# Order of VectorE, of the weight splits and of the last output projection in a two-block transformer kernel

## The reference, cut to what matters

```python
# first block: an even layer (Fourier mix and differential attention), an odd layer (short conv)
x = x + gate0 * (concat(fourier, attention) * silu(g)) @ even_w_out
h = rms_norm(x) ...; bg, cg, xt, g = split(h @ odd_w_in)
x = x + gate1 * (bg * conv3(cg * xt) * silu(g)) @ odd_w_out
# second block: an RG-LRU branch y_a and an HGRN2 branch y_b over one input projection
h = rms_norm(x); xa, ga, q, f, v, g, m_a, m_b = split(h @ w_in)
y = sigmoid(m_a) * y_a + sigmoid(m_b) * rms_norm(hgrn2(silu(q), f, v)) * silu(g)
x = x + y @ w_out
x = x + square(relu(rms_norm(x) @ w_up)) @ w_down
return rms_norm(x)
```

## Time and profile before

| | |
|---|---|
| median of 3 runs | 3000.41 us (2998.44 to 3001.2) |
| the profiled execution's own time | 3001.18 us |
| its span, first to last instruction | 2999.1 us |
| TensorE matmuls busy in the span | 2866.4 us (96%) |
| VectorE, ScalarE, GpSimd busy | 1370.8, 904.8, 615.0 us |
| mean granted TensorE clock | 0.985 of 2.4 GHz |

### The profile page before, as it was taken

The page is one execution under the profiler, slowest core; times in us unless marked ns, Lnnn a source line. Parts: engine busy times, 40 slices in busy tenths (PEclk is TensorE's granted clock), DMA queues, the critical chain, the costliest instruction groups (busy, mean ns, idle before and its releaser), DMA issues.

```text
span 2999.1 us, 34350 instructions
## 1 busy us (share of the span) xinstructions
PE 2866.4 (96%) x14138; PEld 2356.7 (79%) x14138; DVE 1370.8 (46%) x1509; ACT 904.8 (30%) x1013; POOL 615.0 (21%) x316
## 2 busy tenths in 40 slices
PE   6999997989999999899999999999988999999997
PEld 3788765777788888688888888888876888888886
DVE  4478116885622223744435556666656212111126
ACT  4332215663311112344442222222323212021122
POOL 0111113112222223222221111111122222222222
PEclk8999998999999999999999999999999999999999
DMA  6111450012211112111121111111021111111113
GB/s 217 63 36 36 129 159 1 1 45 79 60 49 50 49 50 71 46 49 50 47 59 36 36 36 36 36 36 36 29 58 55 56 43 49 50 50 49 50 50 112
DMA packets 277010, 168.50 MB, mean 56 GB/s; under 512 B 5760, under 2 KB 270336, under 8 KB 276480
## 3 DMA queue, kind: packets, MB, share of 16 engines
q1 hardware_dynamic: 275424, 162.88, 18.3%
q10 hardware_dynamic: 1440, 3.51, 0.3%
HBM read 162.17 MB, written 4.19 MB: 55 GB/s over the span
## 4 chain that ended last, share of the span: by engine, by line
issue 61%; PE 25%; POOL 8%; ACT 3%; DVE 1%; DVEq 1%; POOLq 0%; ACTq 0%
POOL Wlo L398 8%; PE PS L1384 8%; PE PS L1386 7%; PE PS L1385 7%; ACT prob L644 3%; PE PS L1669 2%; DVEq L1101 1%; DVE acol L1097 0%; PE PS L1672 0%; POOLq L402 0%; DVE acol L1102 0%; DVE X L872 0%; PE PS L1690 0%; DVE Rn L866 0%; POOLq L397 0%
## 5 line engine op out<-in xcount | busy, mean ns | idle before, releaser
L398 POOL TENSOR_TENSOR Wlo<-Wraw,Whi 128x1024 fp32r<-128x1024 f32 (+1 forms) x240 | 572.6, 2386 | 2163.2 <-ACT Whi L453 2163.2
L1384 PE MATMUL PS<-Bh,Whi 128*128 128x512 f32 x2176 | 862.9, 397 | 28.6 <-DVE Bl L879 9.6
L1386 PE MATMUL PS<-Bh,Wlo 128*128 128x512 f32 x2176 | 850.9, 391 | 0.0
L1385 PE MATMUL PS<-Bl,Whi 128*128 128x512 f32 x2176 | 850.7, 391 | 0.0
L1384 PEld LDWEIGHTS PS<-Bh,Whi 128*128 128x128 f32 x2176 | 411.1, 189 | 120.4 <-DVE Bl L879 14.3
L1386 PEld LDWEIGHTS PS<-Bh,Wlo 128*128 128x128 f32 x2176 | 410.7, 189 | 86.9
L1385 PEld LDWEIGHTS PS<-Bl,Whi 128*128 128x128 f32 x2176 | 411.4, 189 | 83.4 <-issue 1.0
L1384 PE MATMUL PS<-Hh,Whi 128*128 128x512 f32 x1120 | 444.7, 397 | 13.8 <-POOL Wlo L398 5.8
L1385 PE MATMUL PS<-Hl,Whi 128*128 128x512 f32 x1120 | 436.9, 390 | 0.0
L1386 PE MATMUL PS<-Hh,Wlo 128*128 128x512 f32 x1120 | 436.8, 390 | 0.0
L453 ACT ACTIVATE Whi<-Wraw 128x1024 fp32r<-128x1024 f32 (+1 forms) x240 | 249.5, 1040 | 552.6 <-PE PS L1386 534.2
(11 more groups left out here) (294 smaller groups left out, 2900.3 us busy)
## 6 DMA issues: line engine op xcount, KB each, us to landing
Wraw<-in_w_in SPq DMA_DIRECT2D x64, 512.0 KB, 4.0
Wraw<-in_w_down SPq DMA_DIRECT2D x38, 512.0 KB, 3.8
adaV<-in_ada_w SPq DMA_DIRECT2D x16, 1024.0 KB, 5.1
Wraw<-in_odd_w_in SPq DMA_DIRECT2D x32, 512.0 KB, 4.1
Wraw<-in_w_up SPq DMA_DIRECT2D x32, 512.0 KB, 4.1
Wraw<-in_even_w_in SPq DMA_DIRECT2D x24, 512.0 KB, 3.8
adaW<-in_ada_w SPq DMA_DIRECT2D x8, 1024.0 KB, 8.7
Wraw<-in_even_w_out SPq DMA_DIRECT2D x14, 512.0 KB, 3.9
```

Source lines behind the costliest of these rows:

```text
L398: pool.tensor_tensor(Wlo[:, slot, 0:tiles, :], Wraw[:, slot, 0:tiles, :], Whi[:, slot, 0:tiles, :].bitcast(F32), ALU.subtract).then_inc(lo ...
L1384: mm(out, Whi[:, u % 2, k, :], hi[:, k, c], start=(k == 0), stop=False)
L1385: mm(out, Whi[:, u % 2, k, :], lo[:, k, c], start=False, stop=False)
L1386: return mm(out, Wlo[:, u % 2, k, :], hi[:, k, c], start=False, stop=(k == KT - 1))
```

## The change

1. `projection`, VectorE, n = 9 to 12: the two `scaled` now stand ahead of `add_square`, the two `low` behind it.
2. ScalarE at stage beginnings (`oi`, `rg`, `mlp`): the split of unit u+2 stands right behind the wait for unit u, ahead of the reading of u's accumulator. In `oi` and `mlp` that order holds for all units, in `rg` for the first two of each eight.
3. The last head of the recurrence. TensorE takes y's tiles one by one, each for both output units (`both`). VectorE does the levels 5 and 6 closer together, one low part of y (tile 0) ahead of level 5, tiles 1 and 2 around the last scores, the product of the gates (`gates_in`) after the last scores, tiles 4 to 6 behind the states. ScalarE splits tile 0 and the weights of the second output unit ahead of its last gate, and takes a square root of a small tile before its copy of the keys.

```diff
@@ act_program, oi
             got(act, 0, 2, b)
+            split_next(0, 2, b + 1)
             act.wait_ge(sem("cgs_free"), i + 1)
             act.activation(cgs[:, :], acc(0), COPY).then_inc(acc_free[0], 1)
-            split_next(0, 2, b + 1)
@@ act_program, rg
             for m in range(2):
-                if i or m:
-                    split_next(0, 2, b + m)
+                if i and m == 0:
+                    split_next(0, 2, b)
                 got(act, 0, 2, b + m)
+                split_next(0, 2, b + m + 1)
                 act.wait_ge(sem("xp_free"), i * 2 + (m + 1))
...
             for m in range(2):
-                split_next(0, 2, b + 2 + m, 4 if m == 1 else KT)
+                if m:
+                    split_next(0, 2, b + 3, 4)
                 got(act, 0, 2, b + 2 + m)
@@ act_program, hg
+            if h + 1 == HG_HEADS:
+                y_split(0)
+                split_next(0, 2, BASE["ho"])
             act.activation(hm[:, :], acc(u % 2), ACT.Sigmoid).then_inc(acc_free[u % 2], 1)
...
-        split_next(0, 2, BASE["ho"])
-        for k in range(KT - 1):
+        for k in range(1, KT - 1):
             y_split(k)
+        act.wait_ge(sem("states_ready"), HG_HEADS - 1)
+        act.activation(hroot, hss, SQRT)
         act.wait_ge(sem("kt_psum"), HG_HEADS)
@@ act_program, mlp
-                if c or k:
+                if c and k == 0:
                     split_next(0, 2, u)
                 got(act, 0, 2, u)
+                split_next(0, 2, u + 1)
...
-                if k == 7:
-                    split_next(0, 2, u + 1)
@@ dve_program, projection
                 residual(n)
-                if n:
-                    add_square(n)
                 if 9 <= n < 13:
                     for k in (2 * (n - 9), 2 * (n - 9) + 1):
                         scaled(0, k)
+                if n:
+                    add_square(n)
+                if 9 <= n < 13 and i < 3:
                     for k in (2 * (n - 9), 2 * (n - 9) + 1):
-                        if i < 3:
-                            low(0, k)
+                        low(0, k)
@@ dve_program, hg
+        def gates_in(b):
+            evacuated(dve, 0, 2, b + 4)
+            tt(hm[:, :], hm[:, :], hg[:, :], ALU.mult).then_inc(sem("gm_ready"), 1)
...
-            for lev in range(2, LEVELS):
+            for lev in range(2, 5 if last else LEVELS):
...
-                if lev == 4:
-                    evacuated(dve, 0, 2, b + 4)
-                    tt(hm[:, :], hm[:, :], hg[:, :], ALU.mult).then_inc(sem("gm_ready"), 1)
-                elif lev > 4 and last:
-                    y_low(2 * (lev - 5))
-                    y_low(2 * (lev - 5) + 1)
-            scores_in(h, LEVELS - 2)
+                if lev == 4 and not last:
+                    gates_in(b)
+            if last:
+                y_low(0)
+                z_tile(h, 5)
+                scores_in(h, 3)
+                dve.drain()
+                scores_in(h, 4)
+                decay_on(5)
+                z_tile(h, 6)
+                decay_on(6)
+            else:
+                scores_in(h, LEVELS - 2)
             dve.drain()
...
             if last:
-                y_low(4)
+                y_low(1)
+                scores_in(h, 5)
+                y_low(2)
+                dve.drain()
             scores_in(h, LEVELS - 1)
             dve.drain()
-        y_low(5)
+        gates_in(BASE["hg"] + 5 * (HG_HEADS - 1))
+        y_low(3)
         states(HG_HEADS - 1)
-        y_low(6)
+        for k in range(4, KT - 1):
+            y_low(k)
@@ pe_program, behind the recurrence
+        def both(*ks):
+            for u in (o0, o0 + 1):
+                quad(u, ks, (Bh, Bl), odd_wait)
         level(last, 4)
-        quad(o0, (0, 1), (Bh, Bl), odd_wait)
+        both(0)
         level(last, 5)
-        quad(o0, (2, 3), (Bh, Bl), odd_wait)
         level(last, 6)
         keys_turn(last)
-        quad(o0 + 1, (0, 1), (Bh, Bl), odd_wait)
+        both(1)
         increments(last)
-        quad(o0 + 1, (2, 3), (Bh, Bl), odd_wait)
+        both(2)
         output_rows(last)
-        quad(o0, (4, 5), (Bh, Bl), odd_wait)
+        both(3, 4)
         output_turn(last)
-        quad(o0, (6, 7), (Bh, Bl), odd_wait)
-        quad(o0 + 1, (4, 5, 6, 7), (Bh, Bl), odd_wait)
+        both(5, 6)
+        both(7)
         by_halves(2, o0, (Bh, Bl))
```

More of the change, by code:

```diff
@@ L779, in f_out, with y_split @@
             act.activation(hk[:, :], acc(u % 2), ACT.Sigmoid, scale=-1.0).then_inc(acc_free[u % 2], 1)
+        def y_split(k):
+            act.wait_ge(sem("y_done"), k + 1)
+            act.activation(Bh[:, k, :], Yr[:, k, :], COPY).then_inc(sem("yh_hi"), 1)
         for h in range(HG_HEADS):
@@ L807, in act_program @@
                 f_out(h + 1)
-        split_next(0, 2, BASE["ho"])
-        def y_split(k):
-            act.wait_ge(sem("y_done"), k + 1)
-            act.activation(Bh[:, k, :], Yr[:, k, :], COPY).then_inc(sem("yh_hi"), 1)
-        for k in range(KT - 1):
+        for k in range(1, KT - 1):
             y_split(k)
+        act.wait_ge(sem("states_ready"), HG_HEADS - 1)
+        act.activation(hroot, hss, SQRT)
         act.wait_ge(sem("kt_psum"), HG_HEADS)
```

## The result

The changed kernel takes 2974.9 us (2974.21 to 2975.46, four runs) against 3000.8 for the kernel before in the same session: ratio 0.9914 with an interval of 0.9901 to 0.9927, so 25.9 us faster where 32.2 were forecast. Its profiled execution has a span of 2973.2 us.

A forecast was written before the change was run, and what follows sets the result against it. TensorE, its matmuls busy 96% of the span, was taken as the bound, so only its waits could shrink: 12.6 (norm) + 13.2 (stage beginnings) + 6.4 (last head) = 32.2 us, giving 2968 us, own range 2962 to 2974, overall 2960 to 2982.

The forecast's parts named there:

- Stage beginnings: At `rg`, `mlp` and `oi`, earlier weight splits shorten TensorE's waits: 9.1, 3.2 and 0.9 us saved, sum 13.2.
- Norm: New norm order in three projections: shorter opening waits and 12 matmuls at the higher clock, 4.0 + 4.3 + 4.3, sum 12.6 us.
- Held: Norm: GpSimd's split holds VectorE's scale to its end; scales end 1.25, add 1.9, low parts 3.5 us behind it.
- from 4.27 to 1.8 us: Second projection's opening: TensorE's wait for the norm's low parts shrinks this far, as the opening starts 2.45 us sooner.
- 5.4 us: Norm's loop over GpSimd, ScalarE and VectorE per piece, down from 6.2 us, so TensorE's 5.5 sets the pace.
- less than the 3.51 that left the clock alone: Norm openings: the remaining 1.8 us wait is shorter than one at 2305.41 behind which the clock stayed at 2.4 GHz.
- Last head: Last head of the recurrence, to its second output unit: 45.6 us instead of 52.0, 6.4 saved, with 8.3 of waits left.
- I count none: Last head, 2159 to 2166: no clock loss counted, each wait being under 3.51; if it falls, up to 1.9 us, twice.
- The lag: Rival at the norm: split starts no sooner, only 0.3 per piece won, wait above 4 us; 11.6 lost, 2980; chance 0.08.
- the scales run free: Rival at the norm: scales not held by GpSimd, through before the split ends; 3 x 1.2 us more, 2964; chance 0.07.
- the last head gives nothing: Rival: close levels leave TensorE waiting, the clock falls twice, both units' end costs more; 6.4 us lost, 2974.5; chance 0.07.
- The slower one: Rival at 32 up-projection units: square held, 2.65 instead of 1.23; 3047 us if the chain, about 7, exceeds 11; chance 0.04.

## Why the prediction was right, and where it was off

Direction, mechanism and range held (2974.9 within 2960 to 2982, though 0.9 above the likeliest case's own 2962 to 2974; the likeliest value itself, 2968, was 7 off). Part of the nearness is luck: in the last head a chain priced too dear hid most of a clock that was not counted. Of the 32.2 us 25.9 came.

- **Stage beginnings, 13.2: right.** 0.82, 9.09 and 3.2 in the full change, and the same alone. `rg`'s wait of 7.54 is 0.3, as worked out. That its ten matmuls at the lower clock would go too was right here.
- **Norm, 12.6: the largest miss; 8.2 came.** "Held" was right, and so were 1.25, 1.9 and 3.5 behind the split's end. The term that was mis-sized first is the opening wait, "from 4.27 to 1.8 us"; it is 2.39. The loop was taken as "5.4 us", with a split that keeps its 2.38; but VectorE's low pair laps 0.5 us into the next split, which then takes 2.7, and the loop is 5.7, above TensorE's 5.5. Each opening gains 2.04 instead of 2.45: 1.2 us of the shortfall. The other 3.1 are the clock. I had taken a wait "less than the 3.51 that left the clock alone" for safe, and had the opening's 12 matmuls fall to 2.75 us, from 4.28 in the second projection and from some 4.6 in the others. They took 4.45, 2.85 and 4.43, while before they had taken 5.06, 4.28 and 4.46. The idle matmuls brought back 1.5 and 1.6 at just the two openings that had a fall, which shows it.
- **Last head, 6.4: 4.9 came.** Its waits are 0.2, 1.7, 1.7, 0.2 and 2.3, in all 6.1 instead of 8.3, so the chain of levels, keys and states was priced 2.2 too dear (the states alone 1.0). But "I count none" for the clock was wrong: it fell twice, in level 6 behind its wait of 1.68 (and stayed down through the wait of 1.72), and behind the 2.29. The keys and the six matmuls behind them cost 1.3 more at the lower clock, nine cost 1.6, and a level that takes 2.35 where one at 2.4 GHz takes 1.97 costs 0.4, in all 3.3. 6.4 + 2.2 - 3.3 is 5.3; the remaining 0.4 I can't place. With idle matmuls in these waits 3.1 came back.
- **The end.** The last norm starts 26.5 us sooner and ends 25.9 sooner: ScalarE's wait for the last sum is 2.50 instead of 1.94, with a clock of 0.63 instead of 1.00 while the sum is made. Not forecast, 0.6.
- **The rivals.** The lag did not stay (2.4, not over 4). That the scales run free is refuted by their 2.71 for two. That the last head gives nothing was half right in its mechanism, the clock falls twice, and wrong in its size. The slower one had its condition and not its effect: all 32 squares of `mlp` are held, and its 2.65 for one is the rule now, but nothing waits for them, as the 7 us of 11 said.

The squares' group in the changed kernel (duration ns min/median/max):

```profile
L1381 DVE TENSOR_TENSOR sq<-ut x32: 2606/2614/2700, 2277.4 to 2868.9; 128x1024 f32<-128x1024 f32 x32
```

The Trainium skill, "SBUF — State Buffer", section "SBUF: two separate sides", says that whichever of the two starts first gets the shared port pair for its whole instruction and the other blocks. The prediction used one half of that, VectorE held by GpSimd; the other half, GpSimd held by VectorE, is where the splits' 0.35 us come from, and by it a loop above 5.4 was to be had beforehand. The traces agree with both halves (2.71 for the scales, 2.71 to 2.76 for the split), and with the remark that two SBUF inputs are what matters: the same add takes 0.68 under a split when one input is in PSUM.

## What to carry to other kernels

Before reordering around a hold between VectorE and GpSimd, ask whether one operand of the VectorE instructions can lie in PSUM: here that was worth 20 us in either order, and the reorder of the norm 6 to 8 with the hold and some 1.5 without it. Price a TensorE wait of 1.7 us or more as itself plus 1.3 to 2.6 for a clock that may fall, and take one wait without a fall as nothing more than that. Where such a wait can't be removed, idle matmuls into a free PSUM bank fill it. In a chain of three engines, look for overlap at both ends of each instruction: who holds whom changes as soon as the loop gets shorter.

## What the runs showed of the hardware that I had not expected

- A GpSimd subtraction of 128x1024 that starts while a VectorE pair with two SBUF inputs is running is, in the norm's loop, recorded as *longer* (2.71 to 2.76 instead of 2.40 us for 0.5 of overlap), not as later.
- The clock fell behind waits of 1.7, 2.3 and 2.4 us, and it did not fall behind others of 2.4 and 3.5. The wait of 3.5 at `mlp` kept 1.00 in one kernel and had 0.52 to 0.64 behind it in three that reach it 5, 8 and 18 us sooner. Two profiles of one kernel agree on the places, but the mean clock differs between runs of one kernel. What decides remains open: the length of the wait alone does not.
- Six or eight idle matmuls in a wait of 1.7 to 2.4 us (at the second opening they leave 0.59 us of it) kept the clock at 1.00 behind every wait that had had a fall: two openings and two places in the last head.
